# A diffusion step with a 16-expert layer: output projection tile by tile, router on scaled weights, the last gate's columns computed under the choice of tokens

## The reference, cut to what matters

```python
mod = jax.nn.silu(cond) @ lp["w_ada"] + lp["b_ada"]
shift_a, scale_a, gate_a, shift_f, scale_f, gate_f = jnp.split(mod.astype(x.dtype), 6, axis=-1)
h = rmsnorm(x, lp["norm_mix_g"]) * (1 + scale_a) + shift_a
y, s_f, s_b = token_mixer(h, lp, s0_f, s0_b, seg_len)      # ends in concat([A, B]) @ w_out
x = x + gate_a * y
h = rmsnorm(x, lp["norm_ffn_g"]) * (1 + scale_f) + shift_f
x = x + gate_f * ec_moe(h, lp)
...
probs = jax.nn.softmax((xf @ lp["w_router"]).astype(jnp.float32), axis=-1)
cap = CAPACITY_FACTOR * n // N_EXPERTS                     # 64 latent, 16 context tokens
gate_vals, tok_idx = lax.top_k(probs.T, cap)
xe = jnp.take(xf, tok_idx, axis=0)
```

## Time and profile before

| | |
|---|---|
| runs | 1951.13 us median of 3 (1950.51 to 1953.99) |
| profiled execution | 1953.3 us, its span from first to last instruction 1951.2 us |
| PE busy | 1825.9 us, 94% of the span |
| DVE / ACT / POOL busy | 1564.4 / 1260.8 / 257.0 us |
| HBM | 608.65 MB read, 15.47 MB written, 320 GB/s over the span |
| granted PE clock, mean | 0.975 of full |

### The profile page before, as it was taken

The page is one execution under the profiler, slowest core; times in us unless marked ns, Lnnn a source line. Parts: engine busy times, 40 slices in busy tenths (PEclk is TensorE's granted clock), DMA queues, the critical chain, the costliest instruction groups (busy, mean ns, idle before and its releaser), DMA issues.

```text
span 1951.2 us, 24922 instructions
## 1 busy us (share of the span) xinstructions
PE 1825.9 (94%) x9003; PEld 1259.3 (65%) x9003; DVE 1564.4 (80%) x1244; ACT 1260.8 (65%) x996; POOL 257.0 (13%) x95
## 2 busy tenths in 40 slices
PE   3899799829999999999999999999999999999994
PEld 2677677516666666666666666666666666666663
DVE  5532856368898989898989889898989898989894
ACT  5343543317677777777776767676767677777773
POOL 1000000010030302020211203030303030303000
PEclk9999999959999999999999999999999999999997
DMA  9321543639999999999999999999999999999993
GB/s 358 131 71 65 168 166 129 255 111 339 358 366 385 376 377 375 373 387 370 387 368 385 377 384 369 385 368 385 369 384 370 385 372 383 371 385 372 381 339 125
DMA packets 280922, 624.59 MB, mean 320 GB/s; under 512 B 12357, under 2 KB 45754, under 8 KB 280890
## 3 DMA queue, kind: packets, MB, share of 16 engines
q1 hardware_dynamic: 273594, 598.42, 83.7%
q0 software_dynamic: 6000, 21.01, 3.8%
q10 hardware_dynamic: 1296, 4.72, 0.6%
HBM read 608.65 MB, written 15.47 MB: 320 GB/s over the span
## 4 chain that ended last, share of the span: by engine, by line
PE 91%; DVE 4%; DMA 2%; ACT 2%; issue 1%; SPq 0%; POOL 0%; ACTq 0%; DVEq 0%; POOLq 0%
PE bank L1536 17%; PE bank L1537 17%; PE bank L1540 17%; PE bank L1561 8%; PE bank L1566 8%; PE bank L1562 8%; PE bank L1208 3%; PE bank L1210 3%; PE bank L1209 3%; PE bank L1546 1%; DMA raw<-in_w_ada 1%; DVE w_lo L827 1%; ACT w_hi L568 1%; PE bank L1239 1%; PE bank L1240 1%
## 5 line engine op out<-in xcount | busy, mean ns | idle before, releaser
L1113 DVE TENSOR_TENSOR w_lo<-raw,w_hi 128x2048 fp32r<-128x2048 f32 x528 | 1198.7, 2288 | 130.5 <-ACT w_hi L739 123.9
L739 ACT CAST w_hi<-raw 128x2048 fp32r<-128x2048 f32 x524 | 996.4, 1911 | 188.5 <-PE bank L1540 105.9
L1536 PE MATMUL bank<-w_hi,xe_hi 128*80 128x512 f32 (+1 forms) x1536 | 570.6, 378 | 3.3 <-DVE xe_lo L1131 3.3
L1537 PE MATMUL bank<-w_hi,xe_lo 128*80 128x512 f32 (+1 forms) x1536 | 564.5, 374 | 0.0
L1540 PE MATMUL bank<-w_lo,xe_hi 128*80 128x512 f32 (+1 forms) x1536 | 381.6, 373 | 0.0
L1536 PEld LDWEIGHTS bank<-w_hi,xe_hi 128*80 128x80 f32 x1536 | 227.5, 148 | 102.1 <-DVE xe_lo L1131 3.5
L1537 PEld LDWEIGHTS bank<-w_hi,xe_lo 128*80 128x80 f32 x1536 | 228.0, 148 | 98.6 <-issue 0.5
L1540 PEld LDWEIGHTS bank<-w_lo,xe_hi 128*80 128x80 f32 x1536 | 220.4, 148 | 105.0 <-issue 0.7
L1561 PE MATMUL bank<-w_hi,hT_hi 128*80 128x512 f32 x704 | 277.0, 393 | 0.7 <-DVE hT_lo L1141 0.7
L1562 PE MATMUL bank<-w_hi,hT_lo 128*80 128x512 f32 x704 | 275.5, 391 | 0.0
L532 POOL DMA_INDIRECT acc_dram<-yrow,idx_s x16 | 45.1, 2822 | 1132.8 <-DVE yrow L1150 1132.8
(11 more groups left out here) (209 smaller groups left out, 1300.6 us busy)
## 6 DMA issues: line engine op xcount, KB each, us to landing
raw<-in_w_e_gate SPq DMA_DIRECT2D x176, 1024.0 KB, 10.7
raw<-in_w_e_up SPq DMA_DIRECT2D x176, 1024.0 KB, 10.8
raw<-in_w_e_down SPq DMA_DIRECT2D x176, 1024.0 KB, 10.7
raw<-in_w_ada SPq DMA_DIRECT2D x24, 1024.0 KB, 5.1
raw<-in_w_in SPq DMA_DIRECT2D x8, 1024.0 KB, 5.5
raw<-in_w_out SPq DMA_DIRECT2D x4, 1024.0 KB, 5.0
acc_sb<-acc_dram SPq DMA_DIRECT2D x5, 512.0 KB, 6.2
out<-acc_sb SPq DMA_DIRECT2D x5, 512.0 KB, 3.2
```

The lines of the kernel that those rows point to most:

```text
L739: nc.scalar.copy(hi_slot(j), raw[:, raw_slot(j), :]).then_inc(hi_done, 1)
L1113: nc.vector.tensor_tensor(lo_slot(j), raw[:, raw_slot(j), :], hi_slot(j), ALU.subtract).then_inc(lo_done, 1)
L1536: nc.tensor.matmul(out, xe_hi[:, kk, :], wh[:, k, :], start=kk == 0, stop=False)
L1537: nc.tensor.matmul(out, xe_lo[:, kk, :], wh[:, k, :], start=False, stop=False)
```

## The change

Five things change, all between 285 us and 430 us of the profile.

1. Blocks 10 and 11 of `w_ada` leave `PRE` (32 units instead of 36). They are loaded raw into `ada_raw`, over the place of `mix`, once four tiles are projected, and multiplied in plain float32 by the two conditioning vectors (`gate_rows`) while DVE picks tokens. ACT copies the row pairs, PE spreads them over 80 rows in 4 products, DVE adds the bias that SP has preloaded in `gate_f`.
2. The projection loops over tiles outside, with all four `w_out` units resident: the fourth is split into a place of its own (`w_hix`, `w_lox`). The context tile comes last.
3. The router takes tokens on partitions: `wrt` is multiplied by `scaleF` beforehand (`wrtS`), the shift becomes a row of 16 numbers (`brow`); each tile of `xn2` is turned (8 transpositions), copied, and used as stationary operand of 8 products with 16 columns and one for `brow`. Turning and logits of tile t-1 stand within the projection of tile t. The softmax is a tile's.
4. The rounds of the latent choice start when the four latent tiles are done; the context tile's residual, softmax and choice are put between and behind them. POOL writes each tile to HBM on its own.
5. The ring's slots get a new order (`EXP_SLOTS`), and six units instead of eleven are loaded before the gather; the seventh waits for the gather. POOL's first gather reads its indices from `idxT` without the copy.

```diff
+PRE += [("ada", b, kh) for b in range(ADA_FIRST, ADA_SPLIT) for kh in range(2)]
...
+EXP_SLOTS = (0, 1, 2, 6, 7, 8, 9, 10, 3, 4, 5)
...
+                if n == WOUT0:
+                    sp.wait_ge(g_s1, TILES)
+                    sp.dma_start(gate_f[:, :], b_ada[0:1, 5 * D:6 * D].broadcast_to([SLOTS, D])).then_inc(gate_bias, 16)
...
+                n = j + LEAD
+                if EXP_SLOTS[n % RING] < PRE_RING and n < RING:
+                    sp.wait_ge(lo_done, pre_last(EXP_SLOTS[n]) + 1)
+                elif n == PRE_RING:
+                    sp.wait_ge(wo_ps, 2 * T_LAT)
+                    for q in range(4):
...
+                        load(ada_raw[:, q, :].rearrange("p (k n) -> p k n", k=4), rows(w_ada[0, kh * 512:(kh + 1) * 512, c0:c0 + 512]), ada_in)
+                    sp.wait_ge(unit_used, NPRE)
+                elif n == 5:
                     sp.wait_ge(x2_n, TILES)
-                    sp.wait_ge(acc_out, 32)
-                elif j + LEAD >= RING:
+                    sp.wait_ge(acc_out, 16 * TILES)
+                elif n == 6:
+                    sp.wait_ge(xg_in, 16)
+                elif n >= RING:
                     sp.wait_ge(lo_done, unit(j - RING, 0) + 1)
...
+            def exps(t):
+                act.wait_ge(r_sub, t + 1)
+                nc.scalar.activation(pr[:, t, :], pr[:, t, :], ACT.Exp, accum_out=prs[:, t:t + 1]).then_inc(r_exp, 1)
+
+            square_row(0)
+            for t in range(1, T_LAT):
+                turned_row(t - 1, 0)
+                square_row(t)
+            for t in range(T_LAT - 1):
+                exps(t)
+            turned_row(T_LAT - 1, 0)
+            exps(T_LAT - 1)
+
+            square_row(T_LAT)
...
+            exps(T_LAT)
+            for h in range(2):
+                act.wait_ge(grow_ps, h + 1)
+                nc.scalar.copy(gate_row[:, h, :], bank[2 + h][0:2, :]).then_inc(grow_sb, 1)
...
-                    act.wait_ge(topk, 1)
+                    act.wait_ge(grow_ps, 2)
...
-            low(ADA0 + 15)
 
             for m in range(2 * HEADS):
-                if m == HEADS:
-                    low(WOUT0)
-                    mod_columns(10)
-                    mod_columns(11)
...
+            turned_row(T_LAT - 1)
+            residual(T_LAT, 0)
+            less_max(T_LAT - 1)
+            share(T_LAT - 1)
             dve.wait_ge(r_prT, 1)
...
+            step(nc.vector.tensor_copy(prT[:, 0:L_LAT], bank[6][0:EXPERTS, :]))
+            for r in range(CAP_LAT // 8):
+                best(0, 8 * r, r == CAP_LAT // 8 - 1)
+                if r == 0:
+                    residual(T_LAT, 1)
+                if r == 1:
+                    dve.wait_ge(x2_rt, TILES)
+                    nc.vector.reciprocal(rstd[:, T_LAT:TILES], rstd[:, T_LAT:TILES]).then_inc(x2_rc, 1)
+                if r == 5:
+                    less_max(T_LAT)
+                if r == 6:
+                    share(T_LAT)
+            dve.wait_ge(r_prT, 2)
+            step(nc.vector.tensor_copy(prT[:, L_LAT:NTOK], bank[7][0:EXPERTS, P:2 * P]))
...
             for j in range(-LEAD, -1):
                 low_of(j, 0)
+            dve.wait_ge(gate_bias, 16)
+            for half in range(2):
+                cols = slice(half * 512, half * 512 + 512)
+                dve.wait_ge(gate_ps, 5 + half)
+                nc.vector.tensor_tensor(gate_f[:, cols], gate_f[:, cols], bank[2 + half][0:SLOTS, :], ALU.add).then_inc(gatef_sb, 1)
+            dve.wait_ge(gatef_sb, 2)
             modulate(0, 0)
...
-            pe.wait_ge(gate_sb, 3)
-            ada(10)
             pe.wait_ge(gate_sb, 4)
...
+            every = range(4)
+            for t in range(T_LAT):
+                mixed(t, 0, 0, every)
+                mixed(t, 0, 1, every)
+                if t >= 1:
+                    turn_row(t - 1)
+                mixed(t, 1, 0, every)
+                mixed(t, 1, 1, every)
+                if t >= 1:
+                    logits(t - 1)
+            mixed(T_LAT, 0, 0, every)
+            mixed(T_LAT, 0, 1, range(2))
+            turn_row(T_LAT - 1)
+            mixed(T_LAT, 0, 1, range(2, 4))
+            logits(T_LAT - 1)
+            mixed(T_LAT, 1, 0, every)
+            pe.wait_ge(r_pr, T_LAT)
+            for t in range(T_LAT):
+                last = nc.tensor.transpose(bank[6][0:EXPERTS, t * P:(t + 1) * P], pr[:, t, :], ident)
+            last.then_inc(r_prT, 1)
+            mixed(T_LAT, 1, 1, every)
+
+            gate_rows(0, 0)
+            gate_rows(0, 1)
+            turn_row(T_LAT)
+            gate_rows(1, 0)
+            logits(T_LAT)
+            gate_rows(1, 1)
+            pe.wait_ge(r_pr, TILES)
+            nc.tensor.transpose(bank[7][0:EXPERTS, P:2 * P], pr[:, T_LAT, :], ident).then_inc(r_prT, 1)
             for half in range(2):
...
+                pe.wait_ge(grow_sb, half + 1)
+                for st, lo, hi in ((LAT, 0, CAP_LAT), (CTX, CAP_LAT, SLOTS)):
+                    last = nc.tensor.matmul(bank[2 + half][lo:hi, :], ident[0:2, st:st + 1].broadcast_to([2, hi - lo]), gate_row[:, half, :], start=True, stop=True)
+                last.then_inc(gate_ps, 1)
             pe.wait_ge(topk, 1)
```

More of the change, by code:

```diff
@@ L496, in _ @@
             pool.dma_start(x2[:, T_LAT, :], x_prompt[0]).then_inc(x_back, 16)
[L498 to L511, removed]
+            for t in range(TILES):
+                tok = slice(t * P, (t + 1) * P)
+                pool.wait_ge(wo_ev, 2 * t + 2)
+                pool.dma_start(acc_dram[tok, :], x2[:, t, :]).then_inc(acc_out, 16)
+                pool.wait_ge(x2_n, t + 1)
+                pool.dma_start(xn2_dram[tok, :], xn2[:, t, :]).then_inc(xn2_out, 16)
+            pool.wait_ge(xn2_out, 16 * TILES)
             pool.wait_ge(idx_sb, 2)
-            gather(slice(0, 1), 0)
+            nc.gpsimd.indirect_dma_start(
+                out=xg[:, :], out_offset=None, in_=xn2_dram[:, :],
+                in_offset=bass.IndirectOffsetOnAxis(ap=idxT[:, 0:1], axis=0)).then_inc(xg_in, 16)
             steps0 = n[0]
@@ new lines, in best @@
+            def best(first, s, last):
+                work = prT[:, 0:L_LAT] if first == 0 else prT[:, L_LAT:NTOK]
+                step(nc.vector.max(gv[:, s:s + 8], work))
+                step(nc.vector.max_index(gi[:, s:s + 8], gv[:, s:s + 8], work))
+                if not last:
+                    step(nc.vector.match_replace(work, gv[:, s:s + 8], work, -1.0))
+            residual(0, 0)
+            residual(0, 1)
+            norm2(0)
+            for t in range(1, T_LAT):
+                residual(t, 0)
+                turned_row(t - 1)
+                residual(t, 1)
+                norm2(t)
+                less_max(t - 1)
@@ L1216, in parts @@
             def parts(u, k):
+                if u < NPRE and pre_split(u) == SPLIT:
+                    return [w[:, :].rearrange("p (k n) -> p k n", k=k) for w in (w_hix, w_lox)]
                 a = (u % SPLIT)
@@ L1454, in _ @@
                 last.then_inc(m_ps, 1)
[L1456 to L1461 removed]
+            pe.wait_ge(mod_done, ADA_SPLIT + 1)
+            for k in range(KD):
+                last = nc.tensor.matmul(bank[6][0:2, 0:EXPERTS], modT[:, 24 + k, :], wrt[:, k, :], start=k == 0, stop=k == KD - 1)
@@ new lines, in turn_row @@
+            def turn_row(t):
+                pe.wait_ge(x2_n, t + 1)
+                for q in range(2):
+                    if t >= 1:
+                        if q == 0:
+                            pe.wait_ge(xt_act, t)
+                        else:
+                            pe.wait_ge(xt_dve, t)
+                    for k in range(4):
+                        last = nc.tensor.transpose(bank[4 + q][:, k * P:(k + 1) * P], xn2[:, t, (4 * q + k) * P:(4 * q + k + 1) * P], ident)
+                    last.then_inc(xt_ps, 1)
@@ new lines, in logits @@
+            def logits(t):
+                st = CTX if t == T_LAT else LAT
+                if t == 0:
+                    pe.wait_ge(wrt_set, 2)
+                    pe.wait_ge(brow_set, 1)
+                if t < T_LAT:
+                    pe.wait_ge(xt_act, t + 1)
+                    pe.wait_ge(xt_dve, t + 1)
+                else:
+                    pe.wait_ge(xt_act, t + 2)
+                out = bank[7][:, t * EXPERTS:(t + 1) * EXPERTS]
+                for k in range(KD):
+                    nc.tensor.matmul(out, xT[:, k, :], wrtS[:, st, k, :], start=k == 0, stop=False)
+                nc.tensor.matmul(out, ident[0:2, st:st + 1].broadcast_to([2, P]), brow[:, :], start=False, stop=True).then_inc(lg_ps, 1)
@@ new lines, in gate_rows @@
+            def gate_rows(b, kh):
+                out = bank[2 + b][0:2, :]
+                pe.wait_ge(ada_in, 64)
+                if kh == 0:
+                    pe.wait_ge(wo_ev, 2 * (T_LAT - 1) + b + 1)
+                w = ada_raw[:, 2 * b + kh, :].rearrange("p (k n) -> p k n", k=4)
+                x = silu_c[:, :].rearrange("p (s k) -> p k s", s=2)
+                for k in range(4):
```

(3 more changed lines are left out.)

244 lines of the change are left out of this document (98 added, 146 removed).

## The result

The changed kernel takes 1935.4 us in the median of four runs (1934.6 to 1937.94), the kernel before 1952.23 (1950.51 to 1953.99): a ratio of 0.9916 (0.9901 to 0.9931), faster by 16.8 us. The forecast was 1931.2 us and a gain of 19.9. Of the 4.2 us between the two times 3.1 are missing gain; the other 1.1 is the kernel before, which the forecast took at 1951.13 and these runs at 1952.23. The profiled execution of the changed kernel is the slowest of its four, 1937.94 us with a span of 1936.1.

The account below looks back on a forecast made before the run. PE was taken to bound the expert stage, so an earlier start moves the end one for one. First product at 410.2 instead of 430.1 gives 1951.13 - 19.9 = 1931.2 us, range 1925 to 1938; chance 0.73.

Parts of the forecast that it names:

- The start: Projection start after work leaves PE's list: 309.0 instead of 311.8, a gain of 2.8 us; bounds 306.1 and 311.8.
- The projection with the router inside: Four tiles of 10.9 us with turning and logits between them: tile 3 ends at 359.0, the choice begins 19.8 us earlier.
- Rival (b): Overlap of the router fails, each `turn_row` stalling PE for late norming: 2 us a tile, 8 us, 1939; chance 0.06.
- The choice: DVE's token choice with inserted operations of 2.9 us and a wait of 0.6: 3.5 us longer, ending at 396.3.
- A gap of PE before `gate_rows`: Sign that the prediction is wrong: PE idles before the gate's block; it expected PE to work without a pause there.
- rival (a): Gate's block late, PE waiting for its 4 MB: 3 to 12 us more (1934 to 1943); chance 0.11 in part.
- PE's block under the choice: Gate's products and four wide products beside DVE's choice: 21.5 us, ending at 396.6, late by 0.3 us.
- From the choice to the first product: DVE sets the first modulation at 405.5, then 4.7 us as before: first expert product at 410.2 instead of 430.1.
- The cover: Before the first modulation, DVE's subtractions and `gate_f` additions hide the gather by 1.7 us.
- The bound from above (9.36 us): POOL's gather issue slowed beside DVE's subtractions: turned rows at 410.4, 4.9 us later; 2.72 us was taken instead.
- Rival (c): Transfers bound the expert stage, so ring loading counts: 1952.3, no change, or 1958.9 with a late issue; chance 0.10.
- the prediction's other signs of being wrong: ACT's casts waiting for transfers in the first experts (slack some 10 us), or the stage behind 410 longer than before.

Follow-up runs that it names:

- fill_one: Changed kernel plus 24 transpositions that nobody reads, in PE's gap ahead of the turned heads; 1931.77 us, 0.9898 of the kernel before.
- ada_by_tile: Changed kernel with each of the four raw `w_ada` units loaded once its token tile is projected, not all behind tile 3; 1934.48 us, ratio 0.9909.
- late_ring: Changed kernel with expert weight units 4 to 6 also waiting for the gather, so only three load ahead of it; 1938.73 us, ratio 0.992.
- serial_choice: Changed kernel with the latent choice put behind the context tile's logits, the gate's block beneath it; 1950.35 us, ratio 0.9989.
- no_gate_block: Changed kernel without the loads of `w_ada` blocks 10 and 11 and their 16 products, two short products instead; 1939.15 us, ratio 0.993.
- all_four: Changed kernel with filler transpositions, tile-by-tile `w_ada` loads, `gate_f` additions behind the modulation, and the list turned before the wide products; 1928.99 us, 0.9879.

## Why the prediction was right in kind and 3.1 us too good

Forecast and measurement by the prediction's own marks, the measured ones of the profiled execution with 1.87 taken off:

| mark | forecast | measured | difference added |
|---|---|---|---|
| projection starts | 309.0 | 308.4 | -0.6 |
| tile 3 ends | 359.0 | 360.9 | +2.4 |
| choice starts | 373.2 | 375.6 | +0.5 |
| choice ends | 396.3 | 399.55 | +0.9 |
| first modulation | 405.5 | 408.7 | -0.1 |
| first expert product | 410.2 | 413.3 | -0.1 |

**The start.** Right: the clock fell in the gap ahead of the heads, and `fill_one` shows the lower bound of 9.9 us without that. A second fall, at the first products of the projection, was not foreseen.

**The projection with the router inside: the step that was mis-sized.** The prediction counted tiles at 2.4 GHz, 50.05 us in all; 52.5 were measured. The first 1.5 tiles took 328.35 - 310.27 = 18.1 us where 16.35 were reckoned, 1.7 more. Of these 1.5 are the clock, as the same stretch takes 16.6 us in `fill_one`: the first products are 0.43 us apart instead of 0.23. The rest are the logits, which the prediction had no row for. A group takes 1.69 + 0.32 us in the chain. From its start to that of the next `turn_row` 342.36 - 334.68 = 7.68 us pass, of which half a tile takes 5.45; that leaves 2.2 us a group, against 1.8 taken and an upper bound of 2.3, 0.9 for two groups. `turn_row` takes 0.87, not 0.95. Rival (b) is refuted by the trace, without a run of its own: PE never waits for a normed tile.

**The choice.** The wait for the root is there as forecast (0.62 us against 0.6), and the inserted operations come to 2.4 us instead of 2.9. What was missed is DVE's 1.30 us for the late logits of the context tile. They are late since the 4 MB landed at 380.55, 17.8 us behind tile 3's end, where the prediction reckoned 16: PE idled 1.15 us. A gap of PE before `gate_rows` was one of the prediction's own signs of being wrong. This is rival (a) in a small measure, and `ada_by_tile` shows it: with the loads started earlier the 1.3 are gone.

The rate was not what failed. Stretches of PE in the changed kernel (length, busy, clock, DMA share, GB/s):

```profile
365.00:378.00 13.00, 13.00 (x73) 1.00 1.03 379
378.40:380.40 2.00, 1.04 (x5) 1.00 0.07 27
```

The transfers, with 1.05 MB of POOL's writes among them, ran at 379 GB/s against the 387 reckoned. Then a last part took 2 us more, with the 16 DMA engines busy 0.07 in the mean, about as much as one of them. The prediction had 2.2 us for the start of the loads, with no row named, and nothing for their end. In `fill_one` the same four loads have no such tail, and PE does not wait; where it comes from is open.

**PE's block under the choice.** It ended at 402.0, 0.6 us behind DVE's last operation, where 0.3 was forecast. The two runs that leave the block out show that it also kept PE's clock up: without it the wide products take 7.48 us instead of 3.98. The prediction asked what the block costs, and not what its absence would.

**From the choice to the first product.** Right within 0.2 us in sum: 9.13 and 4.60 against 9.2 and 4.7. DVE releases the modulation, as forecast. The gather's issue took 2.41 us and its landing 2.9 behind that, 5.3 in all where 5.5 were reckoned. The cover is 1.1 instead of 1.7, since the gather starts 1.9 us behind the choice instead of 1.2. The list is turned only 0.1 later than reckoned; the rest is POOL, which starts 0.86 us behind DVE's last copy (402.48 to 403.34) where 0.15 was taken. Why it does is open. The bound from above (9.36 us) did not come.

**Rival (c)** is refuted: `late_ring` sends three units later and the stage behind the first product keeps its 1521 us. PE is busy 1300 us of 1300 in the stage after, and ACT waits for no transfer in the first experts (415 to 600 us), so the prediction's other signs of being wrong did not come. The 378 GB/s of the stage after are, as before, above the 358 of the Trainium skill's page DMA: Bandwidth & Descriptors, section "Bandwidth". The same section gives that figure as each core's part when both cores of a memory domain load, and this kernel runs on one core; so the prediction was wrong to say that page and trace disagree.

## What to carry to other kernels

When a serial section is shortened, price its matrix work at both clocks, and ask of each idle gap of PE which work behind it will run at the lower one: here filling one gap of 5.6 us with unread transpositions was worth 3.6 us, though it brought a fall of the clock in later products that had been spared. Work that seems to be only a load on an engine may be what keeps its successors fast, so leave it out in a run of its own before you count on the saving. And of several items in one queue, issue first the small one that another engine waits for.

## What the runs showed of the hardware that was not expected

- PE's clock went from 2.4 to 1.2 GHz while PE was busy without a pause, in the four wide products (stationary 2 x 64, moving 2 x 512). Stretches of PE alone in `fill_one`:

```profile
390.00:392.00 2.00, 2.00 (x6) 1.00 0.00 0
392.00:394.00 2.00, 2.00 (x5) 0.73 0.00 0
394.00:396.00 2.00, 2.00 (x4) 0.50 0.00 0
```

  They took 3.98 us in the changed kernel, 5.31 in `fill_one`, 5.50 in `serial_choice` and 7.48 in `no_gate_block` and `all_four`. In the last two PE had idled before them (2.7 and 3.4 us), in the others not. In the changed kernel the clock fell as well, but just behind them: it is 1.00 from 401 to 402 us and 0.59 from 402 to 403. What made it fall is open; no run changed these products.
- One fall of the clock went with the next: after the heads were turned at 1.2 GHz, the projection 12 us later began at 1.2 GHz too, although the clock had been at 2.4 GHz from 304 to 309 us. After heads turned at 2.4 GHz (`fill_one`) it did not, with the same 2.54 us of idle time ahead of it.
- Four transfers of 1 MB issued together landed 5.3 to 16.3 us after their issue, the same four issued apart 5.2 to 5.5 us. In the changed kernel the last 2 us of the former moved little: a DMA share of 0.07, 27 GB/s.
